# Four chunks of the last modulation by ScalarE products and accumulating DMAs, and two raw weight buffers instead of three

## The reference, cut to what matters

```python
def ada_modulation(cond, w_ada, b_ada):
    m = jax.nn.silu(cond) @ w_ada + b_ada
    return [p[:, None, :] for p in jnp.split(m, N_MOD, axis=-1)]
...
    sh1, sc1, g1, sh2, sc2, g2 = ada_modulation(cond, w_ada, b_ada)
    h = rms_norm(x, g_norm1) * (1 + sc1) + sh1
    proj = h @ w_in            # q, k, v and the three inputs of a short convolution
    ...
    x = x + g1 * (mixed @ w_out)
    h2 = rms_norm(x, g_norm2) * (1 + sc2) + sh2
    x = x + g2 * ec_moe(h2, w_router, w_gate, w_up, w_down)
```

## Time and profile before

| what | value |
|---|---|
| median of 3 runs | 1527.26 us (1527.1 to 1527.64) |
| the profiled execution: span from first to last instruction | 1525.0 us |
| outside that span, median less span | 2.3 us |
| TensorE busy | 1446.9 us, 95% |
| VectorE busy | 602.3 us |
| ScalarE busy | 255.1 us |
| moved by DMA | 572.48 MB, 375 GB/s over the span |

### The profile page before, as it was taken

One profiled execution on the slowest core, in us unless ns is written; L12 is line 12 of the kernel. 1 busy time (PEld: TensorE's weight loads), 2 busy tenths in 40 slices (PEclk: granted clock), 3 DMA queues, 4 the chain that ended last, 5 costly groups with the idle time before them and its releaser, 6 DMA issues.

```text
span 1525.0 us, 18551 instructions
## 1 busy us (share of the span) xinstructions
PE 1446.9 (95%) x7856; PEld 882.0 (58%) x7856; DVE 602.3 (39%) x1019; ACT 255.1 (17%) x358; POOL 26.7 (2%) x58
## 2 busy tenths in 40 slices
PE   6999999999999999999989989999889899899998
PEld 3667788888889997435435335335335335335433
DVE  4433977978768986101301301301301301211313
ACT  4233223333233223000000000000000000000200
POOL 0000000000000000000000000000000000000000
PEclk9999999999999999999999999999999999999999
DMA  9999688777787659999999999999999999999999
GB/s 374 403 395 325 263 324 316 268 261 260 276 294 273 221 191 366 371 433 434 430 431 433 427 435 431 431 434 428 435 431 430 434 429 435 431 429 431 431 422 349
DMA packets 99263, 572.48 MB, mean 375 GB/s; under 512 B 9532, under 2 KB 54532, under 8 KB 76676
## 3 DMA queue, kind: packets, MB, share of 16 engines
q1 hardware_dynamic: 87824, 520.14, 83.5%
q0 software_dynamic: 6912, 50.33, 8.6%
q10 hardware_dynamic: 4468, 1.14, 0.3%
HBM read 565.02 MB, written 6.55 MB: 375 GB/s over the span
## 4 chain that ended last, share of the span: by engine, by line
PE 66%; DMA 24%; DVE 5%; SPq 2%; issue 2%; ACT 1%; ACTq 0%; DVEq 0%
PE psum L639 64%; DMA ring<-in_w_up 20%; DMA ring<-in_w_ada 2%; SPq L551 2%; DMA res<-in_w_ada 1%; DVE res L1618 1%; DVE w_parts L1508 1%; DMA ring<-in_w_down 1%; PE psum L649 0%; PE psum L825 0%; PE psum L1077 0%; DVE stat L1578 0%; DVE hid L1577 0%; PE psum L1047 0%; DVE mix L1581 0%
## 5 line engine op out<-in xcount | busy, mean ns | idle before, releaser
L639 PE MATMUL psum<-ring,hid 128*64 128x512 f32 x3024 | 679.9, 596 | 54.0 <-DMA ring<-in_w_up 40.2
L639 PEld LDWEIGHTS psum<-ring,hid 128*64 128x64 f32 x3024 | 240.2, 138 | 470.3 <-issue 414.3
L1944 DVE TENSOR_TENSOR hid<-psum,hid 128x512 f32<-128x512 f32 x16 | 11.1, 691 | 516.3 <-PE psum L639 516.3
L639 PE MATMUL psum<-h_parts,w_parts 128*128 128x384 f32 x1152 | 207.3, 337 | 1.3 <-DVE mix L1651 1.3
L639 PEld LDWEIGHTS psum<-h_parts,w_parts 128*128 128x128 f32 x1152 | 199.9, 188 | 5.1 <-issue 2.5
L1508 DVE TENSOR_TENSOR w_parts<-ring,w_parts 128x2048 fp32r<-128x2048 f32 x52 | 119.0, 2289 | 76.4 <-ACT w_parts L1208 76.2
L1208 ACT ACTIVATE w_parts<-ring 128x2048 fp32r<-128x2048 f32 x52 | 99.6, 1916 | 209.0 <-PE psum L639 176.9
L639 PE MATMUL psum<-w_parts,h_parts 128*128 128x512 f32 x432 | 103.9, 395 | 2.8 <-DVE w_parts L1508 1.5
L639 PE MATMUL psum<-ring,early 128*32 128x512 f32 (+4 forms) x694 | 96.4, 536 | 7.8 <-DMA ring<-in_w_ada 6.0
L639 PEld LDWEIGHTS psum<-w_parts,h_parts 128*128 128x128 f32 x432 | 79.5, 188 | 28.5 <-issue 10.3
L639 PEld LDWEIGHTS psum<-early,mix 128*128 128x128 f32 x768 | 86.6, 192 | 9.0 <-issue 9.0
(11 more groups left out here) (216 smaller groups left out, 754.0 us busy)
## 6 DMA issues: line engine op xcount, KB each, us to landing
ring<-in_w_up SPq DMA_DIRECT2D x30, 4096.0 KB, 23.2
ring<-in_w_gate SPq DMA_DIRECT2D x28, 4096.0 KB, 30.4
ring<-in_w_down SPq DMA_DIRECT2D x26, 4096.0 KB, 30.0
ring<-in_w_ada POOLq DMA_DIRECT2D x48, 1024.0 KB, 7.5
ring<-in_w_in SPq DMA_DIRECT2D x36, 1024.0 KB, 8.3
ring<-in_w_ada SPq DMA_DIRECT2D x28, 768.0 KB, 15.6
res<-in_w_ada SPq DMA_DIRECT2D x16, 1024.0 KB, 5.7
ring<-in_w_out SPq DMA_DIRECT2D x16, 1024.0 KB, 5.8
```

Source lines behind the costliest of these rows:

```text
L639: return nc.tensor.matmul(out, lhsT, rhs, start=start, stop=stop, skip_group_check=True)
L1944: tt(by_row, bank[1][:, :].rearrange("p (b a) -> p a b", a=4), by_row, ALU.mult).then_inc(act_ready, 1)
```

## The change

The raw buffers go from three to two, which makes the first half of slot 3 free. It holds two buffers of 128 x 1024 floats. The first four chunks of modulation 5 now go in eight half chunks ("jobs"): GpSimd's queue loads a half chunk, ScalarE multiplies it with the two conditioning columns (one product into the other buffer, one in place), and GpSimd's queue sends both products to two sums in DRAM, as plain writes for the first chunk and as accumulating writes for the other three. After the convolution SyncE loads the two sums (1 MB each) into `added_up`, ahead of the first expert weights, and VectorE adds the twelve other chunks onto them. The events of modulation 5 on TensorE are gone. GpSimd's loops are written out.

```diff
-RAW = 3
+RAW = 2
...
-STREAM = [2, 4, 5]
-HERE = 4
-EVENT_SETS = [[(m, k) for k in range(first, min(first + 2, KC + 1))] for m in STREAM for first in range(0, KC + 1 if m < N_MOD - 1 else HERE, 2)]
+STREAM = [2, 4]
+EVENT_SETS = [[(m, k) for k in range(first, min(first + 2, KC + 1))] for m in STREAM for first in range(0, KC + 1, 2)]
 SETS_Q = [(14, 2)]
 SETS_KV = [(1, 3), (3, 2)]
-SETS_CONV = {s: 3 + n for n, s in enumerate([0, 1, 3, 4, 6, 7, 9, 10, 12, 13, 15, 16, 17, 18, 19, 21, 23])}
+SETS_CONV = {s: 3 + n for n, s in enumerate([0, 1, 3, 4, 6, 7, 9, 10, 12, 13, 15, 16, 17, 18, 19])}
...
-ADDED = range(HERE, KC)
+CARRIED = 4
+HALF = D // 2
+CARRY_JOBS = [(k, half) for k in range(CARRIED) for half in range(2)]
+CARRY_AT = {3 * n + 1: n for n in range(len(CARRY_JOBS))}
+CARRY_LOADS = {2: 0, 5: 1, 7: 2, 9: 3, 11: 4, 13: 5, 15: 6}
+CARRY_ADDS = {4: 0, 6: 1, 8: 2, 10: 3, 12: 4, 14: 5, 17: 6}
+ADDED = range(CARRIED, KC)
 ADDS_AT = {s: 2 for s in (3, 4, 5, 7, 8, 9, 10, 11, 12, 13)} | {2: 1, 14: 3}
-ADA_USES = 2 * KC + HERE + 1
+ADA_USES = 2 * KC + 1
...
-        raw = ring[:, 0:2, :].rearrange("p s n -> p (s n)")[:, 0:RAW * UNIT]
+        raw = ring[:, 0, 0:RAW * UNIT]
...
+        carry_in_buf, carry_out_buf = ring[:, 3, 0:HALF], ring[:, 3, HALF:2 * HALF]
+        carry_sums = nc.dram_tensor("carry_sums", (2, P, D), F32).ap()
...
                 if s in FIRST_AT:
                     sp.wait_ge(unit_used, U_QKV + U_CONV)
+                    if s == min(FIRST_AT):
+                        sp.wait_ge(carry_added, 32 * len(CARRY_JOBS))
+                        for n in range(2):
+                            sp.dma_start(added_up[n], carry_sums[n]).then_inc(carried_back, 16)
                     first_load(FIRST_AT[s])
...
-            def ada_load(m, k, j, added=False):
-
-                if added:
+            def ada_load(m, k):
+                j = k % 2
+                if k - 2 in ADDED and m == N_MOD - 1:
                     pool.wait_ge(add_done, 2 * (k - 2 - ADDED[0]) + 2)
+                elif m == N_MOD - 1:
+                    pool.wait_ge(ada_free, k - ADDED[0] + 2 * KC + 1)
                 else:
                     pool.wait_ge(ada_free, k + (KC * STREAM.index(m) + 1))
-                pool.dma_start(ada_buf[j], ada_rows[bass.ds(k * P, P), m * D:(m + 1) * D]).then_inc(ada_landed[j], 16)
-
-            for m in STREAM[:-1]:
-                with pool.Fori(0, KC // 2) as i:
-                    for j in range(2):
-                        ada_load(m, 2 * i + j, j)
-            for k in range(KC):
-                ada_load(N_MOD - 1, k, k % 2, k - 2 in ADDED)
+                pool.dma_start(ada_buf[j], ada_rows[k * P:(k + 1) * P, m * D:(m + 1) * D]).then_inc(ada_landed[j], 16)
+
+            def carry_add(job):
+
+                k, half = CARRY_JOBS[job]
+                pool.wait_ge(carry_ready, job + 1)
+                for n, rows in enumerate((carry_out_buf, carry_in_buf)):
+                    sums = carry_sums[n][:, half * HALF:(half + 1) * HALF]
+                    if k == 0:
+                        pool.dma_start(sums, rows).then_inc(carry_added, 16)
+                    else:
+                        pool.dma_start(sums, rows, accum_op=ALU.add).then_inc(carry_added, 16)
+
+            def carry_load(job):
+
+                k, half = CARRY_JOBS[job]
+                if job:
+                    pool.wait_ge(carry_added, 32 * job)
+                at = (N_MOD - 1) * D + half * HALF
+                pool.dma_start(carry_in_buf, ada_rows[k * P:(k + 1) * P, at:at + HALF]).then_inc(carry_in, 16)
+
+            for k in range(2):
+                ada_load(STREAM[0], k)
+            for place, events in enumerate(EVENT_SETS):
+                for m, k in events:
+                    if k < KC:
+                        t = KC * STREAM.index(m) + k + 2
+                        if t < 2 * KC:
+                            ada_load(STREAM[t // KC], t % KC)
+                        else:
+                            ada_load(N_MOD - 1, ADDED[t - 2 * KC])
+                if place in CARRY_ADDS:
+                    carry_add(CARRY_ADDS[place])
+                if place in CARRY_LOADS:
+                    carry_load(CARRY_LOADS[place])
+            carry_load(len(CARRY_JOBS) - 1)
+            carry_add(len(CARRY_JOBS) - 1)
+            for k in ADDED[2:]:
+                ada_load(N_MOD - 1, k)
...
-            partition_sums(bank[0], added_up, False, ada_free)
+            pe.wait_ge(mod_read, N_MOD - 3)
+            partition_sums(bank[0], added_up, True, ada_free)
...
+                if s in CARRY_AT:
+                    job = CARRY_AT[s]
+                    k = CARRY_JOBS[job][0]
+                    a.wait_ge(carry_in, 16 * (job + 1))
+                    nc.scalar.activation(carry_out_buf, carry_in_buf, ACT.Copy, scale=cond[:, k, 0:1])
+                    nc.scalar.activation(carry_in_buf, carry_in_buf, ACT.Copy, scale=cond[:, k, 1:2]).then_inc(carry_ready, 1)
...
-                    t = 2 * KC + k
+                    t = 2 * KC + k - ADDED[0]
                     v.wait_ge(ada_landed[t % 2], 16 * (t // 2 + 1))
                     if i < 2:
-                        v.wait_ge(unit_used, U_QKV + U_CONV)
-                        ts(added_up[n], ada_buf[t % 2], cond[:, k, n:n + 1], None, ALU.mult).then_inc(add_done, 1)
+                        v.wait_ge(carried_back, 32)
                     else:
                         v.wait_ge(add_done, i - 1)
-                        stt(added_up[n], ada_buf[t % 2], cond[:, k, n:n + 1], added_up[n], ALU.mult, ALU.add).then_inc(add_done, 1)
+                    stt(added_up[n], ada_buf[t % 2], cond[:, k, n:n + 1], added_up[n], ALU.mult, ALU.add).then_inc(add_done, 1)
```

More of the change, by code:

```diff
@@ L342, in build @@
         x_saved, x_back, chunk_in, add_done_3, summed_3 = sem("x_saved"), sem("x_back"), sem("chunk_in"), sem("add_done_3"), sem("summed_3")
+        carry_in, carry_ready, carry_added, carried_back = sem("carry_in"), sem("carry_ready"), sem("carry_added"), sem("carried_back")
         moe_landed = [sem(f"moe_landed{n}") for n in range(WIDE)]
```

## The result

| | before | after |
|---|---|---|
| median, 4 runs each, side by side | 1527.20 us (1527.10 to 1527.64) | 1600.76 us (1600.21 to 1601.84) |
| ratio, 95% interval | | 1.0484 [1.0472, 1.0496] |
| span of the profiled execution | 1525.0 us | 1599.3 us |
| output projection begins | 452.09 us | 525.52 us |

The kernel is slower by 73.5 us (1600.76 against the 1527.26 that the forecast started from). I had forecast 39.4, 1566.7 us, with a range up to 1586 us: the direction and the place were right, the size was not. Two of all the executions reported here took far longer, 3807.23 us for e10 and 5243.25 us for the kernel before beside e9 to e11; they are in none of the medians of this text and in no ratio.

A forecast was written before the change was run, and what follows sets the result against it. The prediction took TensorE to bound the kernel up to the output projection's end, then DMA streaming. Its terms, -3.5 + 40.9 + 2 = +39.4 us on a span of 1525.0, gave 1566.7 us with 2.3 outside it; range 1542 to 1586.

The forecast's parts named there:

- What bounds the kernel: TensorE from 148 to 590 us, then full DMA engines streaming expert weights, whose 935 us don't change.
- The chunk's load behind the unit's: SyncE's queue, convolution: modulation 3's next chunk goes out only in the step needing it, twelve times; +40.9 us.
- The formula of three blocks: Convolution steps 2-5, 8-11, 14-17: TensorE's loss at VectorE's drains, 12L - 55.7 us, L being a late chunk's landing time.
- The size of L: Landing time of a late modulation 3 chunk: 7.1 us for half, 9.0 for half, so 8.05.
- Their bytes only lengthen L, which the 9.0 covers: Half chunk writes to DRAM: 8 MB written, 6 MB read before; term 0, any longer chunk landing within 9.0 us.
- ScalarE's wait for half chunks: Convolution: products wait for half chunk loads behind GpSimd's pair, counting at the beginning of blocks 2 and 3; +2 us (0-8).
- Events: TensorE after steps 21 and 23: two pairs removed, 2 x 1.74 us on the path, -3.5 us.
- Units: Convolution and q projection: unit loads stay hidden with two raw buffers, 11 us against at least 16; term nothing.
- reading back: SyncE's queue near 457 us: 2 MB of sums, hidden with 10 us of cover; additions' term 0, at most 2.
- The range: Whole kernel: 1542 to 1586 us, taking in most of the smaller loss and both larger rivals' centres.
- Full overlap: Rival: beside GpSimd's pairs, chunks land in 12.1 us in half the steps, 7.1 in the others; 1585 us, chance 12%.
- The rival of slow writes: Accumulating writes hold GpSimd's queue, making ScalarE and TensorE wait: 17 us more, 1584 us, chance 10%.

The follow-up runs named there:

- e10: The changed kernel with only the first of the eight half chunk loads, all sixteen writes kept: 1597.7 us, ratio 1.0457 to the kernel before.
- e9: The kernel before with two raw buffers and 28, 18 and 14 idle identity products ahead of TensorE's waits in steps 6, 12, 18: 1576.7 us.
- e11: The changed kernel with three raw buffers and no half chunks, leaving only the removed events and the reading back: 1523.9 us, ratio 0.9979 to the kernel before.
- e1: The kernel before with two raw buffers instead of three and nothing else of the change: 1577.3 us, ratio 1.0325.
- e4: The kernel before with two raw buffers and the chunk's load put ahead of the unit's in SyncE's loop: 1526.6 us, ratio 0.9990.
- e5: The kernel before with two raw buffers and 50, 35 and 27 idle identity products ahead of TensorE's waits in steps 6, 12, 18: 1583.9 us.
- e3: The changed kernel without its twelve accumulating writes: 1586.6 us, ratio 1.0380 to the kernel before.
- e8: The changed kernel with its accumulating writes turned into plain ones of the same size: 1594.7 us, ratio 1.0443 to the kernel before.
- e12: The changed kernel without the two plain writes of the first half chunk, the third written plainly instead of accumulated: 1598.3 us, ratio 1.0475 to the kernel before.

## Why the prediction was wrong in its size, point by point

- **What bounds the kernel**: right. TensorE up to the end of the output projection, 935 us of streaming behind, unchanged but for 0.8 us.
- **The chunk's load behind the unit's**: right, shown by e1 and e4 from both sides. The formula of three blocks holds in seven kernels to within 1 us, once the clock and ScalarE's wait, both below, and the events are added.
- **The size of L: this step failed.** "Their bytes only lengthen L, which the 9.0 covers" was an assertion without a row. For two raw buffers alone L = 8.05 came close (8.18), in part by luck: I had put 7.1 and 9.0 half and half, and with the same traffic it was 8.60 in e5 and 8.94 in e9. The change's own traffic lifts it to 10.30: 12 x 2.25 = 27.0 us over my term of 40.9. From e1 to e3, that is with half chunk loads and four plain writes, the twelve landings grow by 9.8 us (98.1 to 107.9), most of it in one chunk that lands beside the first two writes (10.0 to 15.8); twelve more writes bring 9.2, their accumulation 6.5. The half chunk loads don't seem to matter here, since without them the sum stays (e10). Each of these sums is of one execution, and two with equal traffic lie up to 9.2 apart; what carries them is that the medians of e3, e8 and after go the same way (8.1 and 6.1 us), and the eight landings beside and without the first writes. I bounded the writes only by whether they end in time, not by what they do to a load that VectorE waits for.
- **The clock: a term that was missing.** The sum had nothing for the matmuls behind a wait. In after they take 6.1 us more, over the last waits of the three blocks together.
- **ScalarE's wait for half chunks**: 2 forecast, 2.9 left over in the sum (VectorE's wait for it is 3.56 us), at the beginning of block 2, where I had said that it counts.
- **Events** -3.5: right, -3.2 together with the reading back. **Units** nothing (e4), **reading back** nothing: right.
- The terms of after: -3.5 + 67.9 + 6.1 + 2.9 = 73.4 us, against -3.5 + 40.9 + 2. Of the 34 us between them 27.0 are the size of L.
- **The range**: its upper end took one rival at a time. Full overlap and what the writes cost are no alternatives to each other: in after both stand in the same sum, with the clock, which was no rival at all, on top. The rival of slow writes had them hold GpSimd's queue; what they did was to lengthen the landings.

## What to carry to other kernels

With fewer buffers, look not at the order in a queue but at the value that each wait in it now waits for, and at what stands behind that wait: here an urgent 1 MB load came one step later without a single line of the queue having moved, and turning two lines took back 68 us. When a load falls on the critical path, price it with all that the change itself puts on the DMA engines, writes above all, and price each wait of TensorE together with the matmuls behind it.

## What was not expected of the hardware

- 1 MB written from SBUF to DRAM beside reads cost 6.5 us of a read's landing (16.1 us in after against 9.6 in e12), at full DMA engines and 308 instead of 379 GB/s.
- Behind a wait of 3 to 12 us, 24 matmuls took 5.8 to 7.2 instead of 4.43 us, at a mean granted clock of 0.58 to 0.75 in those looked at (after, e1, e3, e9).
- With the same traffic L was 8.18 in e1, 8.60 in e5 and 8.94 in e9. The four times of e1 lie 6.4 us apart (1573.59 to 1579.98); but the sixteen of the kernel before, run beside it, lie 5.2 apart, so that late loads make the time itself less certain is not shown.
